# Two of 167 weight pairs loaded as nine transfers: 64 partitions at once, and eight times eight partitions four apart

## The reference, cut to what matters

```python
def moe_swiglu(h, router_w, w1, w3, w2):
    logits = (h @ router_w).astype(jnp.float32)
    top_v, top_i = lax.top_k(logits, TOP_K)
    ...
    y = jnp.zeros_like(h)
    for e in range(N_EXPERTS):
        y = y + gates[..., e:e + 1] * swiglu(h, w1[e], w3[e], w2[e])
    return y
```

## Time and profile before

| | |
|---|---|
| median of 3 runs | 1236.86 us (1236.73 to 1236.99) |
| profiled execution, its own time | 1234.24 us |
| its span | 1232.4 us |
| TensorE matmul busy | 1191.9 us, 97% of the span |
| weight loads into TensorE | 773.2 us, 63% |
| VectorE busy | 432.1 us, 35% |
| bytes moved by DMA | 460.11 MB, mean 373 GB/s |
| pairs loaded whole | 143, 2048 KB each, median 27.5 us from issue to landing |
| half loads and columns | 50, 1024 KB each, median 9.4 us |

### The profile page before, as it was taken

How to read it: one execution, slowest core, us unless ns; L and a number is a source line. 1 busy time by engine, 2 the same in 40 slices (tenths; PEclk the granted TensorE clock), 3 DMA queues, 4 the chain that set the end, 5 groups by cost and what they waited for, 6 DMA issues and landing times.

```text
span 1232.4 us, 33558 instructions
## 1 busy us (share of the span) xinstructions
PE 1191.9 (97%) x15497; PEld 773.2 (63%) x15497; DVE 432.1 (35%) x869; ACT 224.6 (18%) x387; POOL 17.0 (1%) x34
## 2 busy tenths in 40 slices
PE   8999999999999999999999999999999999999787
PEld 6757999999997654454655555555545455544444
DVE  4588699999866101021120020102002101101203
ACT  4374543333443000000000000000000000000002
POOL 0400000000000000000000000000000000000000
PEclk9999999999999999999999999999999989999999
DMA  9963799988847899999999999999999999999993
GB/s 388 375 235 103 277 390 356 354 343 329 331 189 283 336 401 385 427 418 426 425 426 425 425 426 425 426 423 404 403 423 427 425 425 425 426 423 429 425 418 132
DMA packets 41038, 460.11 MB, mean 373 GB/s; under 512 B 4672, under 2 KB 5056, under 8 KB 8128
## 3 DMA queue, kind: packets, MB, share of 16 engines
q1 hardware_dynamic: 39552, 455.77, 90.1%
q10 hardware_dynamic: 1344, 2.16, 0.5%
HBM read 456.81 MB, written 1.11 MB: 372 GB/s over the span
## 4 chain that ended last, share of the span: by engine, by line
PE 67%; DMA 14%; DVE 14%; issue 3%; ACT 1%; SPq 0%; DVEq 0%; ACTq 0%
PE bank L2413 35%; PE bank L2428 16%; DMA held<-in_moe 13%; DVE work L1225 6%; DVE split L1209 4%; PE bank L1954 4%; DMA ring<-in_mixa 2%; PE bank L2026 1%; PE bank L2392 1%; PE bank L1846 1%; PE bank L2382 1%; DVE ring L1499 1%; DVE split L1510 1%; PE bank L2162 1%; DVE work L1223 1%
## 5 line engine op out<-in xcount | busy, mean ns | idle before, releaser
L2413 PE MATMUL bank<-held,work 128*32 128x256 f32 x9408 | 521.0, 382 | 22.5 <-DMA held<-in_moe 13.4
L2413 PEld LDWEIGHTS bank<-held,work 128*32 128x32 f32 x9408 | 314.5, 111 | 234.7 <-issue 49.1
L2428 PE MATMUL bank<-held,moe 128*32 128x512 f32 x2320 | 254.8, 592 | 0.0
L1773 DVE TENSOR_TENSOR moe<-moe,bank 128x256 f32<-128x256 f32 (+1 forms) x84 | 28.2, 385 | 606.6 <-ACT moe L1106 606.6
L2428 PEld LDWEIGHTS bank<-held,moe 128*32 128x32 f32 x2320 | 76.1, 110 | 159.0 <-issue 153.8
L1106 ACT ACTIVATE moe<-bank 128x256 f32<-128x256 f32 (+1 forms) x84 | 24.4, 357 | 736.2 <-PE bank L2413 736.2
L2247 PE MATMUL bank<-split 128*128 128x256 f32 x1024 | 125.4, 283 | 0.9 <-DVE split L1209 0.9
L2247 PEld LDWEIGHTS bank<-split 128*128 128x128 f32 x1024 | 123.8, 192 | 1.7 <-DVE split L1209 1.3
L1209 DVE TENSOR_TENSOR split<-ring,split 128x2048 fp32r<-128x2048 f32 x33 | 75.5, 2290 | 7.4 <-ACT split L999 3.3
L1225 DVE SCALAR_TENSOR_TENSOR work<-ring,condp,work 128x512 f32<-128x512 f32 x98 | 73.7, 752 | 4.2
L999 ACT ACTIVATE split<-ring 128x2048 fp32r<-128x2048 f32 x31 | 59.3, 1914 | 74.9 <-PE bank L2247 72.6
(11 more groups left out here) (286 smaller groups left out, 631.8 us busy)
## 6 DMA issues: line engine op xcount, KB each, us to landing
held<-in_moe SPq DMA_DIRECT2D x143, 2048.0 KB, 27.5
held<-in_moe SPq DMA_DIRECT2D x50, 1024.0 KB, 9.4
ring<-in_ffn SPq DMA_DIRECT2D x16, 2048.0 KB, 8.2
ring<-in_ada SPq DMA_DIRECT2D x28, 1024.0 KB, 7.0
ring<-in_ada SPq DMA_DIRECT2D x10, 2048.0 KB, 10.3
ring<-in_mixout SPq DMA_DIRECT2D x2, 2048.0 KB, 8.7
ring<-in_fnet SPq DMA_DIRECT2D x2, 2048.0 KB, 9.2
ring<-in_mixa SPq DMA_DIRECT2D x2, 1024.0 KB, 15.3
```

Source lines behind the costliest of these rows:

```text
L1773: nc.vector.tensor_tensor(gate_e[:, g, 0:n], gate_e[:, g, 0:n], bank[g][:, n:2 * n], ALU.mult).then_inc(e_hidden, counts_for(light, g))
L2413: last = mm(out[:, :, block, :].rearrange("p z (a r) -> p z a r", a=2), x_group[:, 4 * s + k, j * CAP + g * QUAD:j * CAP + (g + 1) * QUAD] ...
L2428: last = mm(bank[3 + n][c * QUAD:(c + 1) * QUAD, :], hiddenT[phase % 2][:, g, blk * QUAD:(blk + 1) * QUAD], weights[:, s, j, n * 512:(n + ...
```

## The change

Pairs 110 and 145 are loaded by nine transfers in place of one. The first takes partitions 0 to 63. The other eight take eight partitions each: 64 + n, 68 + n, ..., 92 + n for n from 0 to 3, then the same from 96 on. Source and destination are those of before, and all nine raise the same semaphore by 16 each. `loads_into` counts nine for such a pair, so that the counts waited for include all nine. `load` gets the pair's number as a further argument. All other loads, their order and the waits before them stay.

```diff
--- before.py
+++ after.py
@@ -117,6 +117,8 @@
 FIRST_LOOP = UNROLLED * GROUP_PAIRS - 1
 SLOTS = 9
 ODD_IN_HALF = {3: 1, 8: 0}
+SHIFTED = (110, 145)
+SHIFTED_ROWS = (slice(0, 64),) + tuple(slice(at + n, at + 32, 4) for at in (64, 96) for n in range(4))
 BY_HALVES = PAIRS - 1
 END_HALVES = FIRST_LOOP + GROUP_PAIRS - 4
 PAIR_AT = {("up", 0, 0): 0, ("up", 0, 1): 2, ("down", 3): 4, ("up", 1, 0): 5, ("up", 1, 1): 7, ("down", 0): 9,
@@ -473,7 +475,7 @@
 
         def loads_into(slot, lo, hi):
 
-            return len([n for n in range(lo, hi) if n % SLOTS == slot])
+            return sum(len(SHIFTED_ROWS) if n in SHIFTED else 1 for n in range(lo, hi) if n % SLOTS == slot)
 
         def landings(group, j, q):
 
@@ -672,9 +674,10 @@
 
                 return moe_d[e, 2 * q:2 * q + 2].rearrange("a (m s) c -> (a m) s c", s=2)
 
-            def load(slot, e, q):
-
-                sp.dma_start(landed(slot).rearrange("p (s c) -> p s c", s=2), pair_of(e, q)).then_inc(piece_in[slot][0], 16)
+            def load(slot, e, q, n):
+
+                for rows in SHIFTED_ROWS if n in SHIFTED else (slice(0, P),):
+                    sp.dma_start(landed(slot)[rows].rearrange("p (s c) -> p s c", s=2), pair_of(e, q)[rows]).then_inc(piece_in[slot][0], 16)
 
             def load_half(slot, e, q, s):
 
@@ -740,7 +743,8 @@
                     elif (q + PAIRS - SLOTS) % PAIRS not in QUAD_SECOND:
                         sp.wait_ge(e_used, PIECES * i + used_with((q + PAIRS - SLOTS) % PAIRS, 1, q - SLOTS - 1))
                     if q not in by_halves:
-                        load(slot_of_pair(group, j, q), before if q == AHEAD else e, q)
+                        load(slot_of_pair(group, j, q), before if q == AHEAD else e, q,
+                             queue_at(GROUP * group + j, q) if ahead_of_loop(group) else FIRST_LOOP + PAIRS * j + q)
                     elif q in QUAD_SECOND:
                         for s in range(2):
                             for d in (1, 0):
```

## The result

The changed kernel takes 1266.34 us (median of 4 runs, 1264.56 to 1269.31) against 1236.80 for the kernel before beside it: a ratio of 1.0242, interval 1.023 to 1.0255. It is 29.5 us slower where 3.3 us less had been forecast, and far outside the range. The profiled execution took 1264.56 us with a span of 1262.8, 30.4 us more than the span of before.

What follows compares the result with a forecast made beforehand. Loads were taken to bound the kernel from 900 us on, the late half of the DMA engines setting the end. Landings 3.3 us sooner, issues and transfers at nothing: 1236.86 - 3.3 = 1233.6 us, range 1231.5 to 1237.2.

Steps and rivals of the forecast that it cites:

- the forecast's 4.93 us: Time one half of the DMA engines gains and the other loses over both pairs, 2.47 us in each.
- Data moved: Loads of pairs 110 and 145: rows at 0.617 us shift between engine halves, so the last landing comes 3.3 us sooner.
- the four rivals: (a) late half gets rows, 0.14; (b) nothing shifts, 0.15; (c) one-packet transfers cost, 0.07; (d) larger gain, inside own case.
- The two halves of the engines: Where loads run out, eight DMA engines finish by about 1207 us, eight others work on until 1215.4, some 9 behind.
- the plateau: Half rate, 203 GB/s from 1208 to 1212 us where loads run out; to be gone or under 2 us.
- these are the same eight each time: Pairs 110 and 145: each 8-row transfer uses the same eight engines, carrying 12 rows while the others carry 4.
- Rival (a): The late half gets the rows, so the chain's load lands 4.93 us later: 1241.8 us; chance 0.14.
- the instruction queue: Queue q8, about 118 us of engine time, 15 us each on eight engines; claimed to cause the late half's lag.
- Per-transfer cost: Sixteen more transfers on the DMA engines: under 0.05 us each when queued, under 0.8 us in all, taken as 0.
- The estimate of 1266 us: Fixed 2.0 us per DMA paid in series, 1234 + 32 us; the prediction set it aside for queued loads.
- Issues: SP issues nine instead of one, twice: 4.1 us more per pair, covered by 7 us and more of queue; cost nothing.
- One for one: The kernel's end moves as much as the last landing of the load issued at 1162.54, until a later load decides.

Runs made afterwards that it cites:

- the markers: Kernel before with four tiny transfers of 1, 2, 4 and 8 rows of 32 B behind its last loads; 1235.79 us in one execution.
- pair 110: The changed kernel with only pair 110 in nine transfers, pair 145 whole; 1245.81 us, ratio 1.0075 to the kernel before.
- pair 145: The changed kernel with only pair 145 in nine transfers, pair 110 whole; 1254.00 us, ratio 1.0143 to the kernel before.
- two halves: Against the change, pairs 110 and 145 as two transfers each, partitions 0 to 63 and 64 to 127; 1256.56 us, ratio 1.0156 to the kernel before.
- mirrored: The change with halves exchanged: partitions 64 to 127 at once, eight small transfers in 0 to 63; 1258.62 us, ratio 1.0173 to the kernel before.
- eight adjacent: The change with its eight small transfers on eight adjacent partitions each, not four apart; 1274.55 us, ratio 1.0301 to the kernel before.
- every second: The change with every second partition as first transfer and the small ones in odd partitions; 1248.86 us, ratio 1.011 to the kernel before.
- pair 45: The change's nine transfers at pair 45 alone instead of pairs 110 and 145; 1247.21 us, ratio 1.009 to the kernel before.
- copies of 8 rows: Kernel before with four added HBM-to-HBM copies of eight 16 KB rows behind each of pairs 110 and 145; 1239.66 us, ratio 1.0022.
- nine transfers by columns: Kernel before with pairs 110 and 145 each cut by columns into nine transfers of all 128 partitions; 1237.05 us, ratio 1.0002.
- four small copies: Kernel before with four added HBM-to-HBM copies of two rows behind each of pairs 110 and 145; 1237.06 us, ratio 1.0005.
- the cut into every fourth partition: Kernel before with pairs 110 and 145 as four transfers each, of every fourth partition; 1236.24 us, ratio 0.9996.
- the first group: First of ten load groups added alone at the kernel before's end: four loads of 128 partitions; 423 GB/s, median packet 611 ns.

## Why the prediction was wrong

The sum of the holes and of the stragglers comes within 3 us of every kernel. "Rows" is what the stragglers should add by the markers: the forecast's 4.93 us for both pairs less the 2.0 us to spare, 2.9; for one pair 2.47 - 2.0 = 0.5. Measured is the difference of the medians, with the interval of the ratio in us.

| kernel | lost + rows | measured |
|---|---|---|
| the change | 25.3 + 2.9 = 28.2 | 29.5 (28.4 to 31.5) |
| pair 110 | 9.3 + 0.5 = 9.8 | 9.0 (6.4 to 12.1) |
| pair 145 | 13.8 + 0.5 = 14.3 | 17.3 (12.2 to 23.3) |
| two halves | 20.7 + 0 | 19.8 (15.5 to 23.1) |
| mirrored | 17.4 + 2.9 = 20.3 | 21.8 (17.2 to 25.5) |
| eight adjacent | 36.0 + 2.9 = 38.9 | 37.8 (30.3 to 44.3) |
| every second | 8.4 + 2.9 = 11.3 | 12.8 (10.5 to 16.7) |
| pair 45 | 9.0 + 0.5 = 9.5 | 11.2 (7.9 to 14.3) |
| copies of 8 rows | 0 + 2.9 | 2.8 (1.4 to 4.2) |

- **The step that failed** is "Data moved": "A row costs 16384 / 26.6 GB/s = 0.617 us", taken as the price of a row on any engine, whatever else is written. That price holds for transfers over all 128 partitions, which is what the weight loads of before were, and by itself also for eight rows four apart (0.61 us). With 64 partitions in a transfer a row takes 1.28 us, with eight adjacent ones 2.08, and while such transfers run, every row of the queue takes some 1.23. This is 25.3 of the 29.5 us, and none of the four rivals had it. The forecast bounded the cost of a transfer, and never that of a row, although both the 64-row and the 8-row shape stood in no row of before.
- **The two halves of the engines** were read rightly, and so was the effect of the shift on the plateau: it is gone. But "I take it that these are the same eight each time" was followed by the assumption that all eight are early. Six are. Rival (a), which "decides as soon as even one of the late engines is among the eight", is the case that holds, but its 4.93 us took the late ones for the last of all. In the one execution with markers they are not: 2.9 us follow, and 2.8 were measured in isolation. The tail of the change fits: by the markers two engines should run on alone for 5.8 us (from 1207.9 to 1213.7, both 4.93 later), and two do for some 6. Without the hole the change would still have been slower. That the instruction queue holds the late half back was not tested.
- **Per-transfer cost** at nothing: right, shown twice (nine transfers by columns, four small copies). The estimate of 1266 us from the fixed 2.0 us per DMA of the Trainium skill (DMA: Bandwidth & Descriptors, section on the anatomy of one DMA) equals the result by chance: sixteen such terms in series are refuted by the 1237.05 us of the nine transfers by columns. (The section describes transfers issued from GpSimd; these are issued from SP.)
- **Issues**: covered, as said; their pace was not that of the row taken. In the changed kernel the nine of pair 110 start 0.85 us apart (912.6 to 919.4), not 0.51. That this is covered too is argued from the 1237.05 us of the nine by columns, which has as many issues.
- **One for one**: the end followed the last landing as forecast, but upwards. TensorE's busy time in 900:1000 fell from 94.2 to 88.6 us, where a rise by 2 was to be seen.
- **Still open.** First, why a hole is as wide as it is. In the kernel before, the 16 rises of one load's semaphore are spread over some 5 us at pair 110 and 9 us at pair 145. By the ways alone, the two halves of the engines should meet only while one half writes in the other's ways; an estimate for two halves of 64 rows is then 5 and 9 us at half rate, 2.5 and 4.5 us lost, and 8.2 and 12.5 were measured. The ordinary rows of engines that should share no way are slow at once, too. Second, why pair 145 costs more than pair 110 (13.8 against 9.3 lost): the engines are further apart by then, but at pair 45, where they are closest (some 4 us), 9.0 is lost. Third, whether the shared way lies at the destination or at the source, as said above. Only argued, not shown. No run found a version faster than the kernel before; the cut into every fourth partition equals it.

## What to carry to other kernels

Before a transfer is cut by partitions, count the ways that each part reaches: parts that touch all groups of four (every second, every fourth partition) run at full pace, and a pair cut into every fourth partition or by columns cost nothing; contiguous halves run at half rate and eight adjacent rows at a seventh, and they slow the ordinary loads beside them. A DMA share of 1.0 with half the GB/s is the mark of it. To rebalance engines, find out engine by engine who is late (tiny transfers at the tail do it), since the slowest one sets every landing.

## What the hardware showed that was not expected

- The pace of one engine depends on the shape of its transfer: 611, 1280 and 2084 ns for the same 16 KB packet, with one, two and four engines on each way. The Trainium skill (DMA: Bandwidth & Descriptors, section The descriptor swizzle) has for 128 partitions one engine for each port; the 611 ns and 423 GB/s of the first group agree, and the other groups show what follows when the engines outnumber the ports.
- A transfer of eight rows uses eight engines: each engine writes one small packet at the end of a transfer, 16 x 8 = 128 more here, and the page's packets under 512 B rose from 4672 to 4800.
- The early half is not the eight engines that small transfers use: of these eight, five were done by 1206.0 us, one at 1207.9, and two at 1213.6 and 1213.7.
- Where TensorE stood still from 1127.4 on for 7.6 us, the granted clock reads 0.66 from 1130 to 1140, a mean over full speed and the lower of the two levels, and the busy time of the same matmuls grew by 12.0 us in all. The mean clocks give the same: 0.018 of 1262.8 us against 0.009 of 1232.4 us, 11.6 us more. That it does not come on top of the holes, since the transfers set the end, is argued from the sums above.
